# Expert weights in fills of 32 KB per partition: five ring slots in place of ten, the down matrix as two 16 KB loads into one slot

## The reference

```python
def moe_ffn(xn, w_router, b_router, w_gate_up, b_gate_up, w_down, b_down):
    logits = (xt @ w_router + b_router)
    top_v, top_e = lax.top_k(logits, 4)           # 4 of 32 experts for each token
    gate = jax.nn.softmax(top_v, axis=-1)
    ...
    def expert_block(args):
        tok, e = args
        gu = xt[tok] @ w_gate_up[e] + b_gate_up[e]
        g, u = gu[:, :1024], gu[:, 1024:]
        g = jnp.minimum(g, 7.0); u = jnp.clip(u, -7.0, 7.0)
        hmid = (u + 1.0) * (g * jax.nn.sigmoid(1.702 * g))
        return hmid @ w_down[e] + b_down[e]
    ...
```

## Time and profile before

| | |
|---|---|
| median of three runs | 1249.18 us (1248.14 to 1253.43) |
| profiled execution, device time | 1245.94 us |
| its span, first to last instruction | 1244.0 us |
| PE busy | 1191.4 us (96%) |
| DVE, ACT, POOL busy | 287.3, 168.0, 74.7 us |
| read from HBM | 443.60 MB, 357 GB/s over the span |
| mean granted TensorE clock | 0.994 of full speed |

### The profile page before, as it was taken

One profiled execution on the slowest core, in us unless ns is written; L12 is line 12 of the kernel. 1 busy time (PEld: TensorE's weight loads), 2 busy tenths in 40 slices (PEclk: granted clock), 3 DMA queues, 4 the chain that ended last, 5 costly groups with the idle time before them and its releaser, 6 DMA issues.

```text
span 1244.0 us, 13736 instructions
## 1 busy us (share of the span) xinstructions
PE 1191.4 (96%) x6081; PEld 578.5 (47%) x6082; DVE 287.3 (23%) x584; ACT 168.0 (14%) x326; POOL 74.7 (6%) x48
## 2 busy tenths in 40 slices
PE   7899988999999999999999999999999999999996
PEld 4585656565544444444444444444444444443432
DVE  3493353122311111112121111112111111111111
ACT  3221443144100000000000000000000000000001
POOL 0460133021000000000000000000000000000000
PEclk9899999999999999999999999999999999999999
DMA  9715403377899999999999999999999999999994
GB/s 344 244 61 223 124 1 135 135 283 279 371 411 426 427 427 429 427 427 428 427 427 427 428 428 428 426 428 427 427 429 426 428 427 428 429 427 427 427 426 178
DMA packets 44141, 445.56 MB, mean 358 GB/s; under 512 B 6041, under 2 KB 10225, under 8 KB 19409
## 3 DMA queue, kind: packets, MB, share of 16 engines
q1 hardware_dynamic: 41936, 444.37, 85.9%
q10 hardware_dynamic: 2144, 0.30, 0.1%
HBM read 443.60 MB, written 1.05 MB: 357 GB/s over the span
## 4 chain that ended last, share of the span: by engine, by line
PE 76%; DMA 18%; DVE 4%; ACT 2%; issue 1%; SPq 0%; DVEq 0%
PE ps L1559 26%; PE ps L1568 15%; DMA R<-in_w_gate_up 10%; PE ps L1543 9%; PE ps L1426 4%; PE ps L1588 4%; DMA XMT<-in_w_gate_up 3%; DMA XM<-in_w_gate_up 3%; PE ps L1162 3%; PE ps L1197 3%; PE ps L1261 2%; PE ps L1266 2%; PE ps L1361 2%; PE ps L1550 1%; DMA R<-in_w_xkv 1%; PE ps L1219 1%
## 5 line engine op out<-in xcount | busy, mean ns | idle before, releaser
L1559 PE MATMUL ps<-R,convT 128*64 128x512 f32 x1232 | 271.8, 593 | 6.9 <-DMA R<-in_w_gate_up 6.9
L1089 DVE TENSOR_SCALAR A<-ps 128x512 f32<-128x512 f32 x32 | 22.1, 692 | 646.9 <-PE ps L1559 646.9
L1559 PEld LDWEIGHTS ps<-R,convT 128*64 128x64 f32 x1232 | 85.8, 137 | 179.3 <-issue 160.0
L1543 PEld LDWEIGHTS ps<-convT,H 128*128 128x128 f32 x1024 | 123.1, 196 | 25.6 <-issue 25.2
L1568 PE MATMUL ps<-R,A 128*64 128x512 f32 x608 | 134.8, 592 | 0.0
L1543 PE MATMUL ps<-convT,H 128*128 128x64 f32 x1024 | 127.5, 283 | 0.3 <-DVE convT L1044 0.3
L720 ACT ACTIVATE A<-A 128x512 f32<-128x512 f32 x32 | 20.2, 630 | 480.9 <-DVE A L1089 480.9
L1568 PEld LDWEIGHTS ps<-R,A 128*64 128x64 f32 x608 | 42.5, 137 | 78.5 <-issue 77.0
L1588 PE MATMUL ps<-A,convT 64*128 64x512 f32 x256 | 63.6, 615 | 1.4 <-ACT A L724 1.4
L724 ACT COPY A<-ps 128x512 f32<-128x512 f32 x32 | 18.8, 586 | 282.3 <-PE ps L1568 282.3
L1559 PE MATMUL ps<-XMT,convT 128*64 128x512 f32 x208 | 46.9, 593 | 1.8 <-DMA XMT<-in_w_gate_up 1.8
(11 more groups left out here) (276 smaller groups left out, 1091.4 us busy)
## 6 DMA issues: line engine op xcount, KB each, us to landing
R<-in_w_gate_up SPq DMA_DIRECT2D x77, 2048.0 KB, 31.7
R<-in_w_down SPq DMA_DIRECT2D x38, 2048.0 KB, 32.7
QK<-in_w_gate_up SPq DMA_DIRECT2D x13, 2048.0 KB, 32.9
A<-in_w_gate_up SPq DMA_DIRECT2D x13, 2048.0 KB, 30.0
XMT<-in_w_gate_up SPq DMA_DIRECT2D x13, 2048.0 KB, 31.9
XM<-in_w_gate_up SPq DMA_DIRECT2D x12, 2048.0 KB, 32.6
XM<-in_w_down SPq DMA_DIRECT2D x7, 2048.0 KB, 32.7
QK<-in_w_down SPq DMA_DIRECT2D x7, 2048.0 KB, 32.9
```

The source lines that it names most:

```text
L1543: last = mm(bank(X_BANK)[:, m * SLOTS:(m + 1) * SLOTS], H_xg[:, t, j, c, :], sel[:, t, :], start=(t == 0), stop=(t == 1))
L1559: last = mm(bank(b)[s * SLOTS:(s + 1) * SLOTS, :], xg[:, 4 * c + j, :], w[:, c * 2 * FF + at + s * BANK:c * 2 * FF + at + (s + 1) * BANK], ...
```

## The change

The ring becomes five slots of 32 KB per partition (4 MB): two pieces of `R`, then `XQ` (the old `XM` and `QK`, now side by side), the last piece of `R`, and the first 8192 floats of `XA` (the old `XMT` and half of `A`, side by side). One expert is three fills: two of the gate/up matrix (512 rows each, four rows of 8 KB to a partition, one run of 32 KB) and one of the down matrix, as two DMAs of 16 KB runs into the halves of one slot, which raise the slot's semaphore to 32 together. PE waits once for each fill and frees it once. So that four neighbouring rows of the matrix can lie on one partition, the gather takes every fourth float of H in place of every second. The small row for the gain of the expert norm moves to `QK` and is transposed in four pieces in place of two.

```diff
-RING = 10
-FILLS = 6
-GU_FILLS = 4
-SPARE = 3
+RING = 5
+FILLS = 3
+GU_FILLS = 2
+SPARE = 1
...
-        ring = ([QK[:, :]] + [R[:, f * 4096:(f + 1) * 4096] for f in range(4)] + [XM[:, :]]
-                + [R[:, f * 4096:(f + 1) * 4096] for f in (4, 5)] + [A[:, 0:4096], XMT[:, :]])
+        ring = [R[:, 0:8192], R[:, 8192:16384], XQ[:, :], R[:, 16384:24576], XA[:, 0:8192]]
...
-                def fill(e, j, slot):
+                def fill(e, j, slot, done):
 
                     if j < GU_FILLS:
-                        src = w_gate_up[0, e, j * 2 * P:(j + 1) * 2 * P, :].rearrange("o (p c) n -> p (o c n)", c=2)
+                        src = w_gate_up[0, e, j * 4 * P:(j + 1) * 4 * P, :].rearrange("o (p c) n -> p (o c n)", c=4)
+                        sp.dma_start(ring[slot], src).then_inc(done, 16)
                     else:
-                        f = (j - GU_FILLS) * 4 * P
-                        src = w_down[0, e, f:f + 4 * P, :].rearrange("o (p c) n -> p (o c n)", c=4)
-                    return sp.dma_start(ring[slot], src)
+                        for i in range(2):
+                            src = w_down[0, e, i * 4 * P:(i + 1) * 4 * P, :].rearrange("o (p c) n -> p (o c n)", c=4)
+                            sp.dma_start(ring[slot][:, i * 4096:(i + 1) * 4096], src).then_inc(done, 16)
...
-                        if n == 5:
+                        if n == 2:
                             sp.wait_ge(pe_two, TWO["oT", 1])
-                        if n in (6, 7):
-                            sp.wait_ge(pe_xo, n - 3)
-                        if n == 8:
+                        if n == 3:
+                            sp.wait_ge(pe_xo, 4)
+                        if n == 4:
                             sp.wait_ge(act_part, 3)
-                        if n == 9:
                             sp.wait_ge(pe_lg, T)
...
-                H_xg = H[:, :, :].rearrange("p t (j n c) -> p t j c n", j=4, c=2)
+                H_xg = H[:, :, :].rearrange("p t (j n c) -> p t j c n", j=2, c=4)
...
-                    for i in range(FILLS - GU_FILLS):
-                        j = GU_FILLS + i
-                        pe.wait_ge(arrived[ring_slot(k, j)], ring_at(k, j))
-                        down(i, ring[ring_slot(k, j)]).then_inc(freed, 1)
+                    slot = ring_slot(k, GU_FILLS)
+                    pe.wait_ge(arrived[slot], ring_at(k, GU_FILLS))
+                    down(0, ring[slot][:, 0:4096])
+                    down(1, ring[slot][:, 4096:8192]).then_inc(freed, 1)
```

More of the change, by code:

```diff
@@ L76, in parts @@
                 return early.enter_context(nc.sbuf_tensor(name, shape, F32R))
-            R_p = parts("R_p", [P, 24576])
-            XM_p, MK_p = parts("XM_p", [P, 4096]), parts("MK_p", [P, 2048])
-            convT_p = parts("convT_p", [P, 1024])
+            R_p, XM_p = parts("R_p", [P, 24576]), parts("XM_p", [P, 4096])
+            parts("gap_p", [P, 4096 + 12288])
+            MK_p, convT_p = parts("MK_p", [P, 2048]), parts("convT_p", [P, 1024])
         R = sb("R", [P, 24576])
-        XM = sb("XM", [P, 4096])
+        XQ, XA = sb("XQ", [P, 8192]), sb("XA", [P, 12288])
         MK = sb("MK", [P, KC, S])
         convT = sb("convT", [P, CC, S])
-        for part, whole in ((R_p, R), (XM_p, XM), (MK_p, MK), (convT_p, convT)):
+        for part, whole in ((R_p, R), (XM_p, XQ), (MK_p, MK), (convT_p, convT)):
             assert nc.lookup_mloc(part).addr == nc.lookup_mloc(whole).addr
+        XM, QK, XMT, A = XQ[:, 0:4096], XQ[:, 4096:8192], XA[:, 0:4096], XA[:, 4096:12288]
         XS_p, MV_p = XM_p[:, 0:2048], XM_p[:, 2048:4096]
@@ L118, in trunk @@
         trig = sb("trig", [P, 2, T, 32])
-        QK = sb("QK", [P, 4096])
         QA, KA = QK[:, 0:2048], QK[:, 2048:4096]
@@ L253, in trunk @@
         tri = ra[:, 0:P]
-        xg_rows = rb[0:4, 0:256]
-        late = ring[5]
+        xg_rows = QK[0:2, 0:512]
+        late = ring[2]
         gfin = late[:, 0:D]
@@ L348, in ring_slot, with landed @@
             return (FILLS * k + j) % RING
+        def landed(n):
+            return 32 if n % FILLS == GU_FILLS else 16
         def ring_at(k, j):
-            return 16 * ((FILLS * k + j) // RING + 1)
-        def spare_slot(j):
-            return 2 + j % SPARE
+            n = FILLS * k + j
+            return sum(landed(m) for m in range(n % RING, n + 1, RING))
+        SPARE_SLOT = 1
         with nc.Block() as block:
@@ L436, in _ @@
                             sp.wait_ge(freed, n - RING + 1)
-                        fill(slice(k, k + 1), j, ring_slot(k, j)).then_inc(arrived[ring_slot(k, j)], 16)
+                        fill(slice(k, k + 1), j, ring_slot(k, j), arrived[ring_slot(k, j)])
                 sp.wait_ge(freed, FILLS * (E - 1))
@@ L450, in _ @@
                                     sp.wait_ge(g_freed, r * (E * FILLS) + e * FILLS + j + 1)
-                                    fill(bass.ds(e, 1), j, spare_slot(j)).then_inc(g_arr[j % SPARE], 16)
+                                    fill(bass.ds(e, 1), j, SPARE_SLOT, g_arr[0])
                 for t in range(T):
@@ L1175, in transpose_rows @@
                             tr(bank(7)[:, 0:R_END], prm_rows[:])
-                            xg_gain = xg_rows.rearrange("j (n c) -> j c n", c=2)
-                            for c in range(2):
-                                last = tr(bank(7)[:, R_XG + 4 * c:R_XG + 4 * (c + 1)], xg_gain[:, c, :])
+                            xg_gain = xg_rows.rearrange("j (n c) -> j c n", c=4)
+                            for c in range(4):
+                                last = tr(bank(7)[:, R_XG + 2 * c:R_XG + 2 * (c + 1)], xg_gain[:, c, :])
                             last.then_inc(pe_prm, 1)
@@ L1532, in _ @@
                 last.then_inc(pe_cnt, 1)
-                H_xg = H[:, :, :].rearrange("p t (j n c) -> p t j c n", j=4, c=2)
+                H_xg = H[:, :, :].rearrange("p t (j n c) -> p t j c n", j=2, c=4)
                 def gather(sel):
-                    for c in range(2):
-                        for j in range(4):
-                            m = 4 * c + j
+                    for c in range(4):
+                        for j in range(2):
+                            m = 2 * c + j
                             for t in range(T):
@@ L1554, in gate_up @@
                 def gate_up(j, xg, w):
-                    for c in range(2):
+                    for c in range(4):
                         for b, at in ((G_BANK, 0), (U_BANK, FF)):
                             for s in range(2):
-                                last = mm(bank(b)[s * SLOTS:(s + 1) * SLOTS, :], xg[:, 4 * c + j, :],
+                                last = mm(bank(b)[s * SLOTS:(s + 1) * SLOTS, :], xg[:, 2 * c + j, :],
                                           w[:, c * 2 * FF + at + s * BANK:c * 2 * FF + at + (s + 1) * BANK], start=False,
-                                          stop=(j == 3 and c == 1), skip_group_check=True)
+                                          stop=(j == 1 and c == 3), skip_group_check=True)
                     return last
@@ L1657, in _ @@
                                 bias(O_BANK, 2 * FF, g_bsel)
-                                for i in range(FILLS - GU_FILLS):
-                                    j = GU_FILLS + i
-                                    pe.wait_ge(g_arr[j % SPARE], r * (32 * E) + e * 32 + 16 * (j // SPARE + 1))
-                                    down(i, ring[spare_slot(j)]).then_inc(g_freed, 1)
+                                pe.wait_ge(g_arr[0], r * (64 * E) + e * 64 + 64)
+                                down(0, ring[SPARE_SLOT][:, 0:4096])
+                                down(1, ring[SPARE_SLOT][:, 4096:8192]).then_inc(g_freed, 1)
                                 pe.wait_ge(g_o, r * E + e + 1)
```

8 lines of the change are left out of this document (3 added, 5 removed).

## The result

The changed kernel takes 1427.72 us (median of 6 runs, 1420.82 to 1429.19), beside 1250.44 us for the kernel before on the same chip (6 runs). The ratio is 1.1403, with a 95% interval of 1.138 to 1.1427. Forecast were 1252.5 us and a range that ended at 1262. The profiled executions are 1244.0 us and 1418.8 us from first to last instruction: +174.8 us to explain.

A forecast was written before the change was run, and what follows sets the result against it. The prediction took the DMA weight stream to set the time from about 899 us, up to expert 30's fourth gate/up fill, then PE's work. Terms +3.4 - 3.9 + 3.4 + 0.4 = +3.3 us gave 1252.5 us, range 1246 to 1262.

The forecast's parts named there:

- Start of the run: At expert 0, the first fill waiting for a freed slot goes out after 32 matmuls, at 327.83 us: +3.4 us.
- Rate: In the weight stream, 32 KB runs save a fixed part per run over 58 gate/up fills: -3.9 us.
- no saving: Rival on the weight stream: engines treat 32 KB runs as 16 KB pieces, +7.2 us, 1256.4 us; chance 15%.
- slower long runs: Rival on the weight stream: long runs slower by 2% say, 11.4 us on top of 7.2, 1267.8 us; chance 7%.
- price per DMA: Faster rival: 64 fewer DMAs each save a price, PE becomes the bound, its 11.5 us of waits go, 1237.7; 5%.
- the slowest engine catches up: Rival on the DMA engines: fewer, longer runs take away the lag between landings, 3.5 us go, 1249.0 us; chance 6%.
- PE behind the deciding fill: At expert 30's last gate/up fill, PE has 32 matmuls after the landing in place of 16: +3.4 us, paid once.
- The gather: Its 32 weight loads per expert at every fourth float cost up to 0.45 us more; +0.4 us in the sum.
- It is hidden in all but the one gather: PE at 28.5 us per expert stays under the stream, so only the gather behind the deciding fill costs: +0.4 us.
- Slower through the gather: Rival at the gather: loads take twice 0.119 us, PE becomes the bound, about +110 us, 1359 us; chance 5%.

The follow-up runs named there:

- e1: Changed kernel with only the gather's step set back to every second float of H: 1250.1 us, ratio 1.0003 to the kernel before.
- c4: c3 with down fills issued and awaited by freed halves, and the last two experts' fills awaited by halves: 1251.68 us, ratio 1.0016.
- e7: e1 with each 4 MB gate/up fill as two DMAs with runs of 16 KB: 1256.71 us, ratio 1.0071 to the kernel before.
- e6: Kernel before with the gather and the transposes of the hidden rows both reading contiguous floats: 1245.01 us beside 1244.44.
- c3: Changed kernel with H copied once, sorted, for a contiguous gather; expert 0 keeps 16 KB runs and every second float: 1255.64 us, ratio 1.0057.
- e2: Kernel before with one edit, the gather reading H at every fourth float: 1425.07 us, ratio 1.1404.
- e9: Kernel before with the gather reading H at every third float: 1349.43 us in one run.
- e5: Changed kernel with the gather in two halves of 8 matmuls, one behind each gate/up fill: 1404.24 us in one run.
- e8: Kernel before with its gather at every second float spread over the gate/up matmuls, one behind each pair: 1494.83 us in one run.
- e3: Changed kernel with one gather matmul behind each pair of gate/up matmuls of the expert before: 1616.65 us, ratio 1.2933.

## Why the prediction was wrong

**Start of the run: the issue came as worked out, the cost is small.** In e1 the first fill that waits for a slot is issued 333.40 - 321.44 = 11.96 us after the gather of expert 0; the fill that it was to fall in with stands 327.83 - 315.87 = 11.96 us after it in the kernel before (315.87 is the start of that gather there), and the one that it replaces 3.4 us ahead of that. c4 adds a point: undoing this alone brings 0.4 us, since another fill is next in line.

**Rate: right, as far as one execution of each kernel tells.** 430 GB/s for 427, and 4.6 us between e7 and e1 where 3.9 were put. The rivals of no saving and of slower long runs fall. So does the price per DMA, which would have ended PE's waits for fills: e1 issues four DMAs per expert in place of six, and its PE still waits 14.2 us for fills. That the slowest engine catches up is not seen either: the landings at 956.79 and 1192.97 in e1 are 29.52 us per expert apart, where 430 GB/s allow 29.26.

**PE behind the deciding fill: right.** In e1 the deciding fill of expert 30 lands at 1192.97, 871.5 us after the first gather; in the kernel before 1188.08 - 315.87 = 872.2. Start and rate together gave -0.5, measured are -0.7. From there to the end it is 1252.3 - 1192.97 = 59.3 us against 1244.0 - 1188.08 = 55.9: +3.4. From first gather to the end e1 takes 930.9 us, the kernel before 928.1: +2.8, where these three terms and no gather gave +2.9. That the two meet so closely is luck in part. Another execution with the fills of before (e6) takes 929.5 us for this stretch, 1.4 more than before, and the medians say less: e1 has a ratio of 1.0003 (0.998 to 1.0025), where +2.9 us would be 1.0023, and c3, with the same stretch of 930.8 us, has 1.0057.

**The gather: this step failed, by taking over the price of a transpose.** The prediction had: "I take the upper end, since the transposes are the nearest row", 32 x 0.014 = 0.45 us. Measured are 3.70 us on each of 32 gathers. The transposes read at the same step, but the price of their loads is not that of the gather's. In the kernel before they follow each other so:

```profile
1195.37 0.60 PEld L1162 LDWEIGHTS ps<-ident,A 128*128 128x128 f32 x4
```

With 0.21 us for the last load, that is (0.60 - 0.21) / 3 = 0.13 us from load to load. Three loads at the gather's 0.233 us would need 0.70 us, and here 0.39 pass. So these loads are not slow ones hidden behind the transposes' matmuls: they are quicker. By e6 the step of four costs a transpose 0.012 us (0.121 for 0.109), and a load of the gather 0.121 (0.233 for 0.112). Why the one pays a tenth of the other, no run shows.

The trace of before held a warning that was not read, the duration of these loads: 219 ns against 143 for contiguous rows, half as much again, and e6 confirms that the step was what it showed. But it was no price either, since the pace of the gather's loads doubled. For the 0.233 us the gather itself had to be run at this step.

From this, two further sentences fell. "It is hidden in all but the one gather" needed less than 1.4 us per gather, and 3.7 is above it, so PE became the bound. And the Trainium skill ("Advanced Engine Details and Errata", SBUF Cachelines), by which two hits on a 16-byte line are needed to cover the access time, was put aside for want of "a cliff". For the loads of the gather the runs agree with it: 0.118 us at two hits per line and 0.233 at one. For the transposes the penalty is hardly there, 0.121 us at one hit per line.

**The rival that came true was priced too low.** "Slower through the gather" had the place, the point of decision (43 ns per load) and nearly the price of a load (double), and gave 1359. It took 3.8 us per expert and lacked the clock: 2.07 us more per expert on transposes and scatter, through the half clock at the end of each long gather. 31.9 us per expert became 34.1. Nothing in the kernel before showed it: its gathers last 3.8 us and the clock is 1.00 from 403 to 899 us. Nor was the rival's chance of 5% what its evidence was worth, with a written rule for it and only four transposes against it.

## What to carry over

Do not carry the price of an operand's layout over from one kind of instruction to another, as here from transposes to ordinary matmuls. Look at the duration of the loads beside their pace: where only one of the two grows, the price is not known yet, and a run with that one edit, like e2, settles it. When a stage that issues many loads for few columns grows longer, look at the granted clock behind it: part of the price can be paid by other instructions. And compare the price with the slack of the engine that pays it (1.4 us per expert here) as a range up to the dearest row, before calling it hidden.

## What the runs showed of the hardware

- A weight load of the gather, 128 floats per partition, follows the one before by 0.112, 0.118, 0.175, 0.233 and 0.238 us at steps of 1, 2, 3, 4 and 8 floats, or about 1.82 ns per 16-byte line, and not under 0.11. At half the clock the pace at every fourth float is the same, 0.233 us.
- The same step of four costs a transpose hardly anything: 0.121 us from one to the next, against 0.109 for contiguous rows.
- With gathers of 7.5 us the granted clock is at half for 6.8 us in each expert (from 409.4 us, for one), although PE has no gap; with 5.6 us (e9) it falls in each expert too. With one gather of 3.8 us per expert of quick loads (before, e1) it does not. With two of 3.8 us of slow loads (e5) it falls in 24 of 30 experts, so the length of a single gather does not decide it alone.
- Gather matmuls set in pairs between gate/up matmuls on 64 columns cost 0.28 us more per pair than apart, with loads of 0.118 us (e8) and of 0.233 us (e3).
- Runs of 32 KB stream at 430 GB/s, those of 16 KB at 427, in line with the earlier trace rows.
